# Second attention's values by key chunk in a ring, and both attentions' outputs split by GpSimd from a ScalarE copy

## The reference, cut to what matters

```
def windowed_gqa(q, k, v, sink):          # "A"
    for each block i of 128 queries:      # keys of blocks i-1, i, i+1
        sc = q_i @ k^T * scale - slopes * dist      # masked beyond 128
        p = softmax([sc, sink])[..., :-1]
        y_i = p @ v
def neighborhood_attn(q, k, v, rpb):      # "B", a grid of 8 rows x 64 columns
    for each query: 8 rows x 16 columns of keys around it
        p = softmax(q @ k^T * scale + bias)
        y = p @ v
merged = g_a * (y_a @ w_proj_a) + g_b * (y_b @ w_proj_b)
```

## Time and profile before

| what | us |
|---|---|
| median of 3 runs | 1453.21 |
| lowest, highest | 1453.06, 1454.81 |
| the profiled execution | 1455.19 |
| its span, first to last instruction | 1453.4 |
| PE busy in the span | 1440.3 |
| DVE, ACT, POOL busy in the span | 783.5, 611.2, 358.9 |
| attention, from PE's first scores to its last values | about 111 to 201 |

### The profile page before, as it was taken

The page is one execution under the profiler, slowest core; times in us unless marked ns, Lnnn a source line. Parts: engine busy times, 40 slices in busy tenths (PEclk is TensorE's granted clock), DMA queues, the critical chain, the costliest instruction groups (busy, mean ns, idle before and its releaser), DMA issues.

```text
span 1453.4 us, 18730 instructions
## 1 busy us (share of the span) xinstructions
PE 1440.3 (99%) x7061; PEld 1204.6 (83%) x7061; DVE 783.5 (54%) x1306; ACT 611.2 (42%) x960; POOL 358.9 (25%) x361
## 2 busy tenths in 40 slices
PE   9999999999999999999999999999999999999999
PEld 7888888888888888888888888888888888888887
DVE  5648864444443434334478795444446879543432
ACT  5436862234332323233434695343333469533221
POOL 3004521011000000000406785121120678510000
PEclk9999999999999999999999999999999999999999
DMA  5564332323322322322232124223323202322232
GB/s 197 83 127 118 105 109 91 112 87 100 107 95 87 110 92 87 115 87 87 73 117 64 30 60 115 88 87 94 110 73 111 71 30 59 112 92 87 87 103 71
DMA packets 161952, 135.60 MB, mean 93 GB/s; under 512 B 35848, under 2 KB 153872, under 8 KB 161872
## 3 DMA queue, kind: packets, MB, share of 16 engines
q1 hardware_dynamic: 161712, 134.47, 31.1%
q10 hardware_dynamic: 160, 0.07, 0.0%
HBM read 124.23 MB, written 2.92 MB: 87 GB/s over the span
## 4 chain that ended last, share of the span: by engine, by line
PE 93%; DVE 3%; ACT 1%; POOL 1%; issue 1%; DVEq 0%; ACTq 0%; POOLq 0%
PE G L1995 72%; PE G L1977 3%; PE G L2419 3%; PE S L1977 3%; PE T L2086 3%; PE G L2110 2%; PE G L2117 2%; PE G L2207 1%; DVE sq L1572 1%; POOL t L875 1%; PE G L2383 1%; PE G L2161 1%; PE G L2043 1%; ACT w L1076 1%; POOL z L971 0%
## 5 line engine op out<-in xcount | busy, mean ns | idle before, releaser
L1995 PE MATMUL G<-gx,w 128*128 128x512 f32 x2928 | 672.3, 390 | 1.3 <-DVE w L1435 1.3
L1995 PEld LDWEIGHTS G<-gx,w 128*128 128x128 f32 x2928 | 548.6, 188 | 116.8 <-DVE w L1435 2.0
L1435 DVE TENSOR_TENSOR w<-raw,w 128x2048 fp32r<-128x2048 f32 (+3 forms) x109 | 247.9, 2274 | 226.0 <-ACT w L1076 225.8
L1076 ACT ACTIVATE w<-raw 128x2048 fp32r<-128x2048 f32 (+2 forms) x111 | 206.0, 1855 | 142.4 <-PE G L1995 109.6
L1995 PE MATMUL G<-kvb,w 128*128 128x512 f32 x960 | 218.4, 389 | 0.0
L1995 PEld LDWEIGHTS G<-kvb,w 128*128 128x128 f32 x960 | 180.2, 188 | 37.4
L875 POOL TENSOR_TENSOR t<-t,rden 128x512 f32<-128x512 f32 (+2 forms) x128 | 108.9, 852 | 112.9 <-DVE rden L1578 110.9
L917 POOL TENSOR_TENSOR t<-sig 128x512 f32<-128x512 f32 x24 | 35.4, 1473 | 338.1 <-DVE sig L1646 338.1
L1015 POOL TENSOR_TENSOR sumsq_f<-sumsq_f,sq_f 128x512 f32<-128x512 f32 x7 | 9.1, 1300 | 333.4 <-ACT sq_f L1106 333.4
L1709 DVE TENSOR_TENSOR x<-G,x 128x512 f32<-128x512 f32 x48 | 33.1, 689 | 103.2 <-PE G L1995 103.2
L1138 ACT ACTIVATE t<-sq,nm 128x512 f32<-128x512 f32 (+3 forms) x128 | 80.1, 626 | 16.9 <-DVE nm L1572 16.4
(11 more groups left out here) (257 smaller groups left out, 1862.0 us busy)
## 6 DMA issues: line engine op xcount, KB each, us to landing
raw<-in_w_in SPq DMA_DIRECT2D x98, 512.0 KB, 7.6
raw<-in_w_up SPq DMA_DIRECT2D x32, 512.0 KB
raw<-in_w_down SPq DMA_DIRECT2D x32, 512.0 KB
raw<-in_w_out SPq DMA_DIRECT2D x24, 512.0 KB
raw<-in_w_attn_proj SPq DMA_DIRECT2D x8, 512.0 KB
raw<-in_w_fourier_proj SPq DMA_DIRECT2D x8, 512.0 KB
biasb<-bias_rows SPq DMA_DIRECT2D x24, 128.0 KB
xin<-in_x SPq DMA_DIRECT2D x4, 512.0 KB, 6.9
```

Source lines behind the costliest of these rows:

```text
L1076: nc.scalar.activation(high, cut(K.raw[:, j % 2, 0:n]), ACT.Copy).then_inc(K.w_hi, 1)
L1435: nc.vector.tensor_tensor(low, cut(K.raw[:, s, 0:n]), high.bitcast(F32), ALU.subtract).then_inc(K.w_lo, 1)
L1995: mm = nc.tensor.matmul(b[:, :], w(p, k), x(q, k), start=(k == i == 0), stop=(k == kts - 1 and i == len(PASSES) - 1))
```

## The change

Two things change, both in the attention of the first block.

1. **Values of B by key chunk.** Key chunk k of a head of B is seen by two of its four blocks: chunk 1 by blocks 0 and 1, chunk 2 by 1 and 2, chunk 3 by 2 and 3, chunk 0 by 3 and 0 (a ring). `values` now takes a chunk times the transposed probabilities of its two blocks in three passes, so a head takes 4 x 3 = 12 passes of 256 columns and not 18. The first call does chunks 1 and 2, the second 3 and 0. Chunk 2 needs block 2's low part, so a wait for it stands inside the first call. `pt` holds a whole head of B in a buffer, no place is left to clear, and `clear_b` goes.
2. **Outputs.** ACT copies the 64 rows, unrounded, to a new SBUF tile `head_f`, and its `y_all` frees the bank. When both heads of a pair are there, POOL writes the high part (`out_high`, an addition of zero) and the low part (`out_low`) for 128 rows at once: high behind P(4h + 8), low behind P(4h + 9), h the odd head. ACT's copy for the next pair waits for the low part (`y_lo`). DVE's 16 `out` go. In B the reordering of columns moves from ACT and DVE to POOL's reads.

```diff
+    def turned_block(self, n, part):
+        _, e, i, lo, hi = self.where(n)
+        if self.at(n) == "B":
+            return self.K.pt["B"][n // TT % 2][:, part].rearrange("p k e c -> p (k e) c")[:, B_UNITS[i], :]
+        return self.K.pt[self.at(n)][n // 2 % 2][:, part, lo:hi, n % 2, :]
...
             if A.at(n) == "A" and n == 1:
                 clear_a()
-            if A.at(n) == "B":
-                b = n - HEADS * TT
-                if b == 1:
-                    clear_b(0)
-                if b == 3:
-                    clear_b(1)
...
+            if A.kind != "L":
+                for late, part in ((2, out_high), (3, out_low)):
+                    h = A.last_of(n - late)
+                    if h is not None and h % 2 == 1:
+                        part(A, h)
...
+    def out_high(A, h):
+        pool.wait_ge(K.y_all, h + 1)
+        nc.gpsimd.tensor_tensor(out_part(A, h, 0), A.in_order(h, K.head_f[:, :]),
+                                A.in_order(h, K.zeros[:, :].broadcast_to([P, SEQ])), ALU.add).then_inc(K.y_hi, 1)
+    def out_low(A, h):
+        pool.wait_ge(K.y_hi, h // 2 + 1)
+        nc.gpsimd.tensor_tensor(out_part(A, h, 1), A.in_order(h, K.head_f[:, :]),
+                                out_part(A, h, 0).bitcast(F32), ALU.subtract).then_inc(K.y_lo, 1)
...
-            nc.scalar.activation(A.rows(h, q[r, 0, t, :]), A.in_order(h, A.out_bank(h)[r, :]),
-                                 ACT.Copy).then_inc(K.y_hi, 1)
+            if h >= 2 and e == 0:
+                act.wait_ge(K.y_lo, h // 2)
+            nc.scalar.activation(K.head_f[r, :], A.out_bank(h)[r, :], ACT.Copy).then_inc(K.y_all, 1)
...
-            if A.kind != "L" and A.last_of(n) is not None:
-                out(A.last_of(n))
...
             elif m % 2 == 0:
-                pe.wait_ge(K.tile_out, A.g_out(h).value() - 1)
+                pe.wait_ge(K.y_all, h - 1)
...
+            if kind == "B":
+                columns, pt = b[:, :].rearrange("p (i c) -> p i c", c=P), K.pt["B"][h % 2]
+                for k in ((1, 2), (3, 0))[m % 2]:
+                    if k in (2, 3):
+                        pe.wait_ge(K.pt_lo, (U + 4 * h + k + 1).value())
+                    for p, q in PASSES:
+                        mm = nc.tensor.matmul(columns[:, B_COLUMNS[k], :], K.vb[:, p, k, t * P:(t + 1) * P], pt[:, q, k, :, :],
+                                              start=(k == 1 and p == q == 0), stop=(k == 0 and p == 1), skip_group_check=True)
+                mm.then_inc(K.pv_done, 1)
+                return
```

More of the change, by code:

```diff
@@ L59 @@
 B_CHUNKS = ((0, 2), (1, 3), (1, 3), (2, 4))
+B_UNITS = (slice(0, 3, 2), slice(3, 5), slice(5, 7), slice(7, None, -6))
+B_COLUMNS = (slice(0, None, 3), slice(0, 2), slice(1, 3), slice(2, 4))
 B_BIAS = (0, 1, 1, 2)
@@ L76 @@
 J_L, JL = 57, 28
-G_X, G_IN, G_A, G_B, G_MERGE, G_OUT, G_MLP = 0, 8, 26, 34, 42, 74, 82
-G_L, GL = 146, 108
+G_X, G_IN, G_A, G_B, G_MERGE, G_OUT, G_MLP = 0, 8, 26, 26, 26, 58, 66
+G_L, GL = 130, 108
 F_X, F_IN, F_MERGE, F_OUT, F_MLP = 0, 8, 26, 58, 66
@@ L267, in allocate @@
     K.biasb = at("biasb", 77, [P, 2, 3, KH * WINDOW], F32)
+    K.head_f = at("head_f", 72, [P, SEQ], F32)
     K.sig1 = at("sig1", 74, [P, 4, SEQ], F32)
@@ L377, in allocate @@
     K.y_hi = semaphore("y_hi")
+    K.y_all = semaphore("y_all")
+    K.y_lo = semaphore("y_lo")
     K.z_in = [semaphore(f"z_in{i}") for i in range(2)]
@@ L540, in pairs, with block_free @@
         return self.u0 // 2 + m + 1
+    def turned_block(self, n, part):
[3 more added lines that the diff above has]
+        return self.K.pt[self.at(n)][n // 2 % 2][:, part, lo:hi, n % 2, :]
+    def block_free(self, n):
+        h = n // TT
+        if self.at(n) == "B":
+            return self.pairs(2 * HEADS - 2 if h == HEADS else 2 * (h - 2) + 1)
+        return self.pairs(n // 2 - 2)
     def last_of(self, n):
@@ L884, in probabilities, with out_part @@
                 z_summed(A.layer, SUM_AT.index(n))
+            if A.kind != "L":
[3 more added lines that the diff above has]
+                        part(A, h)
             if A.at(n) == "A" and n == 1:
                 clear_a()
-            if A.at(n) == "B":
-                b = n - HEADS * TT
-                if b == 1:
-                    clear_b(0)
-                if b == 3:
-                    clear_b(1)
+        if A.kind != "L":
+            out_high(A, A.total // TT - 1)
+            out_low(A, A.total // TT - 1)
+    def out_part(A, h, part):
+        q = K.qa if A.at(h * TT) == "A" else K.qb
+        return A.rows(h, q[:, part, h % HEADS // 2, :])
+    def out_high(A, h):
[6 more added lines that the diff above has]
+                                out_part(A, h, 0).bitcast(F32), ALU.subtract).then_inc(K.y_lo, 1)
     def clear_a():
@@ L897, in clear_a @@
         nc.gpsimd.memset(K.pt["A"][1][:, :, 1, 1, :].bitcast(F32), 0.0).then_inc(K.pt_zero, 1)
-    def clear_b(i):
-        pool.wait_ge(K.pv_done, HEADS * TT // 2 - 1 + i)
-        nc.gpsimd.memset(K.pt["B"][i][:, :, 3 * i, 1 - i, :].bitcast(F32), 0.0).then_inc(K.pt_zero, 1)
     def scaled_x(k):
@@ L1176, in attention @@
                 exps(n + 2)
-            m, e = n // 2, n % 2
             _, _, _, lo, hi_ = A.where(n)
             act.wait_ge(K.trans_full, (U + n + 1).value())
-            if A.pairs(m - 2).due():
-                act.wait_ge(K.pv_done, A.pairs(m - 2).value())
-            nc.scalar.activation(K.pt[A.at(n)][m % 2][:, 0, lo:hi_, e, :],
+            if A.block_free(n).due():
+                act.wait_ge(K.pv_done, A.block_free(n).value())
+            nc.scalar.activation(A.turned_block(n, 0),
                                  K.T[(U + n) % 2][:, 0:(hi_ - lo) * P].rearrange("p (k c) -> p k c", c=P),
@@ L1578, in rden @@
             nc.vector.reciprocal(K.rden[:, c], K.den[:, c]).then_inc(K.rden_ok, 1)
[L1580 to L1586, removed]
         def low(n):
-            m, e = n // 2, n % 2
             _, _, _, b0, b1 = A.where(n)
             dve.wait_ge(K.pt_hi, (U + n + 1).value())
-            nc.vector.tensor_tensor(K.pt[A.at(n)][m % 2][:, 1, b0:b1, e, :],
+            nc.vector.tensor_tensor(A.turned_block(n, 1),
                                     K.T[(U + n) % 2][:, 0:(b1 - b0) * P].rearrange("p (k c) -> p k c", c=P),
-                                    K.pt[A.at(n)][m % 2][:, 0, b0:b1, e, :].bitcast(F32), ALU.subtract).then_inc(K.pt_lo, 1)
+                                    A.turned_block(n, 0).bitcast(F32), ALU.subtract).then_inc(K.pt_lo, 1)
         if A.kind == "L":
@@ L1624, in attention @@
             split(Num(J_MERGE + 1))
-            out(total // TT - 1)
     def merge(sig, dst, j, g, f, h, mix, sig0, pair_, first=None):
@@ L2094, in values @@
             _, _, _, b0, b1 = A.where(2 * m + 1)
-            kind, cleared = A.at(2 * m), m - HEADS * TT // 2
+            kind = A.at(2 * m)
             b = A.out_bank(h)
@@ L2098, in values @@
                 bank(A.g_out(h))
+            elif m % 2 == 0 and h < 2:
+                pe.wait_ge(K.tile_out, G_A - 1 + h)
             elif m % 2 == 0:
-                pe.wait_ge(K.tile_out, A.g_out(h).value() - 1)
+                pe.wait_ge(K.y_all, h - 1)
             out = b[:, m % 2 * 2 * P:(m % 2 + 1) * 2 * P].rearrange("p (e c) -> p e c", e=2)
@@ L2104, in values @@
                 pe.wait_ge(K.pt_zero, m + 1)
-            if kind == "B" and cleared < 2:
-                pe.wait_ge(K.pt_zero, 2 + cleared + 1)
+            if kind == "B":
[8 more added lines that the diff above has]
+                return
             if kind == "L":
@@ L2115, in values @@
                 for p, q in PASSES:
-                    v = {"A": lambda: K.va[:, p, k, :], "B": lambda: K.vb[:, p, (k + m % 2) % TT, t * P:(t + 1) * P]}[kind]()
-                    mm = nc.tensor.matmul(out[:, :, :], v, K.pt[kind][m % 2][:, q, k, :, :], start=(i == p == q == 0),
+                    mm = nc.tensor.matmul(out[:, :, :], K.va[:, p, k, :], K.pt[kind][m % 2][:, q, k, :, :], start=(i == p == q == 0),
                                           stop=(k == b1 - 1 and (p, q) == PASSES[-1]))
@@ L2173, in merge @@
             for m in range(2):
+                if g.k == G_MERGE:
+                    pe.wait_ge(K.y_all, 2 * HEADS - 1 + m)
                 fm(g + 2 * b + m, wcol(j + b, m), gx)
@@ L2259, in heads_ready @@
     def heads_ready():
-        pe.wait_ge(K.tile_out, G_B + HEADS)
+        pe.wait_ge(K.y_lo, HEADS)
     for i in range(4):
```

1 line of the change is left out of this document (removed).

## The result

The changed kernel takes **1457.32 us** (median of 11 runs, 1455.08 to 1457.81), the kernel before on the same chip 1454.81 us (11 runs, 1452.74 to 1455.49). The ratio is **1.0016, 95% interval 1.0008 to 1.0023**: a small loss, inside the 0.2% that the prediction called no change, and inside its range. Its point, 1453.9, was 0.7 us above its base; the loss is 2.3 (by the ratio) to 2.5 (by the medians).

A forecast was written before the change was run, and what follows sets the result against it. It took a loop through all five engines, not PE's 99% busy share alone, as the bound. B -0.4, A +0.4 and the end +0.7 summed to +0.7 us on the median 1453.21: 1453.9 us, range 1449.3 to 1458.5.

The forecast's parts named there:

- gain and price cancel: Whole kernel: the forecast's own case, 1452 to 1456 us, chance 0.55.
- the end's: After head 13's copy: last transposes at 6.32 and the slab's split at 7.02, costing +0.7 us.
- B was -0.4: Attention B: two heads take 9.35 us against 9.47, -0.12 three times.
- A was +0.4: Attention A: the reciprocal's gain of 0.48 given back by POOL's two insertions, +0.15 a pair, three pairs.
- Step (f): B's first values call: chunk 2 newly waits for block 2's low part, PE idle 0.7 to 1.0 us a head.
- the half behind an odd head's copy: Loop of B: from an odd head's copy to the next copy, 5.07 us.
- POOL's prices: Output split on POOL: high 1.04 us, low 1.29, nothing extra for reordered columns.
- Rival 2: POOL in B too slow on reordered reads, 2.8 us each for high and low: 9 us slower, 1463; chance 0.15.
- the 4.35 called PE's and unchanged: Attention A: stretch from the first call behind the pair's split to the next copy, 4.35 us as before.
- step from the last transposes to the split: End of the attention: the weight slab's split starts 0.70 us after the last transposes.
- Rival 1, PE-bound: Values of B: low part in time and POOL hidden, so passes are won, -5.7 and +0.7: 1448.2 us; chance 0.2.
- Rival 3: A and the end cost more: P(13) and P(14) each half a microsecond later, +2 more, 1456 us; chance 0.1.

The follow-up runs named there:

- Outputs alone: Kernel before with only the outputs split by GpSimd, B keeping its 18 passes a head; median 1456.34 us, ratio 1.0010 against the kernel before.
- PE busy in the gap: Changed kernel plus eight unused passes in PE's idle time before the weight slab; median 1455.93 us, ratio 1.0005 against the kernel before.
- before, gap widened: Kernel before with the sigmoid table load moved ahead of the slab's split, lengthening PE's wait; median 1458.36 us, ratio 1.0022.
- Chunk 2 late: Changed kernel with chunk 2's three passes moved behind the transposes of the next head's first block; median 1455.39 us, ratio 1.0006 against the kernel before.

## Why the prediction was right, and where it wasn't

The forecast said that gain and price cancel, and the time lies in its range (put on the forecast's own base, the ratio gives 1455.5, inside its 1452 to 1456). In part that is luck. Of its three terms only the end's had the right sign: B was -0.4 and came out +0.45, A was +0.4 and came out -0.25, and these two errors nearly cancel. In the ratio's terms the point was 1.6 us too low (+0.7 against some +2.3), mostly by something that it left out, the clock.

- **B: the wait is right, a size is wrong, and with it the sign.** Step (f) put PE's idle time before chunk 2 at 0.7 to 1.0 us a head. In the trace it is 0.90 for the first head, then 0.31 to 0.33 behind an even head's copy and 0.62 to 0.63 behind an odd one's, 3.7 in all (5.2 in the weight loads' rows). It is shorter because PE's work ahead of it ends 1.51 behind the copy (181.89) and not at 0.9. Two heads were to take 9.35; they took 9.64. The mis-sized term is the half behind an odd head's copy, 5.07 worked out and 5.37 measured. The working is for an odd head's copy but took ACT's times from the one at 178.16, which is head 10's, an even one: exponential at 0.50, high part at 0.99. Behind the odd head's copy at 182.68 in the same trace they come at 0.61 and 1.24:

```profile
183.29 0.51 ACT L1138 ACTIVATE t<-sq,nm 128x256 f32<-128x256 f32 x1
...
183.92 0.38 ACT L1182 ACTIVATE pt<-T 128x256 fp32r<-128x256 f32 x1
```

In the changed kernel they come at 0.62 and 1.25 (180.38, 181.00, 181.63 above). With 0.26 more the half comes to 5.33 and two heads to some 9.6, a loss of about 0.4 and not a gain. The other half was 4.27, not 4.13. Moving the three passes took 0.44 off two heads.

- **POOL's prices: right.** High 1.04, low 1.28 to 1.30, no surcharge for reordered columns. Rival 2 is out. By the estimate that the rival took from the Trainium skill (GPSIMD Engine Reference, § 7, Performance pitfalls; some 102 cycles for each small read command), a reversed operand of 32 runs of 16 would have cost 2.7 us more. The trace doesn't agree, at least not that each run is a command of its own: B's 1.28 stands beside A's 1.30.
- **A: wrong sign.** +0.15 a pair was forecast, -0.03 to -0.05 measured (heads 5 to 7 and the start bring it to -0.25 in all). Up to the call behind the pair's split the working is right: 6.83, and 6.86 in the trace (139.75 to 146.61). The step that failed is the last, the 4.35 called PE's and unchanged: it was 4.14 (146.61 to 150.75). Before, transposes in it stood behind a P that ended at 150.22 (they start at 150.28, the next scores at 150.58), because DVE had its output of the pair's even head (148.79, 0.68 us) ahead of the reciprocal (149.39); after, that P ends at 147.32, and the transposes start at 148.00, the next scores at 148.14.
- **The end: right.** +0.7 forecast, +0.90 measured (the last transposes at 6.52 behind head 13's copy, not 6.32). *Outputs alone* shows that it is POOL's work ahead of P(62). The prediction's step from the last transposes to the split (0.70) is exact in the trace: 196.54 and 197.24.
- **The term that failed by being absent: the clock.** The prediction said that PE's idle time before the slab would be longer than 1.30 and priced it at nothing beyond the shift. It was 2.02, and the 48 passes behind it cost 1.58 more. *PE busy in the gap* removes it, *before, gap widened* produces it.
- **Rival 1, PE-bound:** out. Two heads of B took 9.64, and 9.20 without the wait, 12 passes fewer for 0.27 less than before. **Rival 3** had the right side and about the right size for the wrong reason: A came out shorter and the end only 0.2 above the forecast; the clock did it.

*Chunk 2 late* has the clock at 1.00 in its profiled execution and a window 2.84 shorter than after's (1.31 of it in B), but its median is only 1.9 lower. The mean granted clock of each execution explains most of it. Its three executions on the lower level all have 1.000 and take 1452.29 to 1452.57, 2.8 less than after's on that level (1455.08 to 1455.43). On the upper level four have 0.999 and take 1454.84 to 1455.42, and five have 0.997 or 0.998 and take 1455.88 to 1456.29: it looks as if the clock fell in these five and not in the others. They have no trace, so that stays unshown.

Left open: why PE's wait in the second block is 0.29 us shorter behind the change, and what makes ACT's next instruction come later behind an odd head's copy than behind an even one's.

## What to carry to other kernels

Before counting a saved pass, look at what the engine waits for behind it: here a third of the value passes went, and the time reappeared as a wait for a low part in the loop and as idle time before a weight slab at the end. When work is merged so that it needs a later operand, place it where that operand is already there; that alone was worth 0.44 us in two heads. When a duration is taken from a row, take it from an instruction of the same kind of place: here an even head's row stood for an odd head, and the 0.26 us turned the sign of a term. And price an idle gap of TensorE not only by its length: read the granted clock in the windows behind it, since a gap that grew from 1.30 to 2.02 us made unchanged passes 1.58 us slower.

## What the runs showed of the hardware

- The granted clock fell to the level of 1.2 GHz behind idle times of PE of 2.02 and 2.81 us (windows of 0.53 and 0.61, 0.50 and 0.68). It did not in the profiled executions behind 1.29, 1.30, 1.51 and 1.86, and not where eight passes filled the gap. The price was 1.58 and 1.45 us in 48 passes: about the same for either gap.
- Every kernel's executions stand on two levels some 2 us apart with nothing changed; the profiles with the lower clock at 8 to 16 us are those whose first scores come at 110.8 to 111.6, the others have them at 108.95 and 109.22.
- In all twelve profiles, ACT's next exponential starts 0.49 to 0.50 us behind the start of an even head's 64x512 copy from PSUM and 0.61 to 0.62 behind an odd head's (heads 1 to 13), whether or not ACT had waited in front of the copy. The two differ in the bank and in the 64 rows; which of them does it, no run shows.
